# Stick-breaking attention: sums of softplus by matmul replaced by scans of sigmoids along rows, with the weights turned by TensorE

## What is computed

```
z = einsum('bhqd,bhsd->bhqs', q_blk, k) * HEAD_DIM ** -0.5
visible = arange(T)[None, :] < q_pos[:, None]
neg_log_1m_beta = where(visible, softplus(z), 0.0)
between = cumsum(neg_log_1m_beta, axis=3, reverse=True) - neg_log_1m_beta
weights = where(visible, exp(log_sigmoid(z) - between), 0.0)
out = einsum('bhqs,bhsd->bhqd', weights, v)
...
merged = sigmoid(gate_sb) * (o_sb @ w_branch_sb) + sigmoid(gate_rw) * (o_rw @ w_branch_rw)
h = h + rms_norm(merged @ w_out)
f = rms_norm(h); h = h + rms_norm((silu(f @ w_ffn_gate) * (f @ w_ffn_up)) @ w_ffn_down)
```

## Time and profile before

| | us |
|---|---|
| median of 3 runs | 879.5 (879.44 to 879.79) |
| the profiled execution | 879.9, its span 878.0 |
| PE busy | 862.6 (98%) |
| DVE busy | 487.1 (55%) |
| ACT busy | 411.1 (47%) |
| POOL busy | 94.1 (11%) |
| mixing stage on PE, from its first step to `u0.U` | 183.2 to 376.7 |

### The profile page before, as it was taken

How to read it: one execution, slowest core, us unless ns; L and a number is a source line. 1 busy time by engine, 2 the same in 40 slices (tenths; PEclk the granted TensorE clock), 3 DMA queues, 4 the chain that set the end, 5 groups by cost and what they waited for, 6 DMA issues and landing times.

```text
span 878.0 us, 18916 instructions
## 1 busy us (share of the span) xinstructions
PE 862.6 (98%) x8165; PEld 717.7 (82%) x8165; DVE 487.1 (55%) x642; ACT 411.1 (47%) x572; POOL 94.1 (11%) x92
## 2 busy tenths in 40 slices
PE   6999999999999999999999999999999999999997
PEld 5999999877777777767888898888888888888886
DVE  6459997346766666529675754444444444322333
ACT  6445565369777777555343643333333333211331
POOL 2015544111011101043100000000000000000000
PEclk9999999999999999999999999999999999999999
DMA  9332223321210011222367323333333333323311
GB/s 281 102 97 73 77 68 97 121 62 56 73 47 17 26 40 39 75 96 73 96 216 270 89 69 100 96 96 96 96 96 97 96 98 100 99 91 105 100 77 72
DMA packets 109584, 82.82 MB, mean 94 GB/s; under 512 B 3471, under 2 KB 100025, under 8 KB 109258
## 3 DMA queue, kind: packets, MB, share of 16 engines
q1 hardware_dynamic: 109514, 81.77, 30.4%
HBM read 75.99 MB, written 5.77 MB: 93 GB/s over the span
## 4 chain that ended last, share of the span: by engine, by line
PE 93%; DVE 4%; issue 1%; ACT 1%; DMA 0%; DVEq 0%; SPq 0%
PE psum L592 47%; PE psum L1899 19%; PE psum L1622 8%; PE psum L1678 7%; PE psum L1824 2%; PE psum L1942 2%; PE psum L1513 1%; PE psum L1834 1%; PE psum L1805 1%; DVE w_lo L582 1%; PE psum L1853 1%; DVE shift_diff L1184 1%; PE psum L1504 1%; DVE k_mod L1225 1%; DVE v_t L1189 1%
## 5 line engine op out<-in xcount | busy, mean ns | idle before, releaser
L582 DVE TENSOR_TENSOR w_lo<-w_raw,w_hi 128x1024 fp32r<-128x1024 f32 x69 | 88.9, 1289 | 120.7 <-ACT w_hi L577 116.3
L592 PE MATMUL psum<-f_hi,w_hi 128*128 128x512 f32 x336 | 130.8, 389 | 0.0
L592 PE MATMUL psum<-f_lo,w_hi 128*128 128x512 f32 x336 | 130.7, 389 | 0.0
L592 PE MATMUL psum<-f_hi,w_lo 128*128 128x512 f32 x336 | 130.7, 389 | 0.0
L1096 ACT ACTIVATE w_hi<-w_raw 128x1024 fp32r<-128x1024 f32 x44 | 46.7, 1061 | 166.7 <-PE psum L592 159.4
L1459 DVE TENSOR_TENSOR w_lo<-w_raw,w_hi 128x1024 fp32r<-128x1024 f32 x44 | 53.9, 1226 | 125.6 <-ACT w_hi L1096 121.4
L577 ACT ACTIVATE w_hi<-w_raw 128x1024 fp32r<-128x1024 f32 x70 | 73.7, 1054 | 74.7 <-PE psum L1899 56.1
L592 PE MATMUL psum<-h_hi,w_hi 128*128 128x264 f32 (+2 forms) x400 | 98.2, 310 | 0.8 <-DVE w_lo L582 0.8
L592 PE MATMUL psum<-h_lo,w_hi 128*128 128x264 f32 (+2 forms) x400 | 96.5, 306 | 0.0
L592 PE MATMUL psum<-h_hi,w_lo 128*128 128x264 f32 (+2 forms) x400 | 96.5, 306 | 0.0
L592 PEld LDWEIGHTS psum<-f_hi,w_hi 128*128 128x128 f32 x336 | 63.1, 188 | 13.2
(11 more groups left out here) (314 smaller groups left out, 1655.8 us busy)
## 6 DMA issues: line engine op xcount, KB each, us to landing
w_raw<-in_w_in SPq DMA_DIRECT2D x30, 512.0 KB, 3.7
w_raw<-in_w_g SPq DMA_DIRECT2D x22, 512.0 KB, 3.7
w_raw<-in_w_u SPq DMA_DIRECT2D x22, 512.0 KB, 3.8
w_raw<-in_w_d SPq DMA_DIRECT2D x22, 512.0 KB, 3.5
w_raw<-in_w_in SPq DMA_DIRECT2D x48, 128.0 KB, 2.2
w_raw<-in_w_out SPq DMA_DIRECT2D x8, 512.0 KB, 5.0
kept_gates<-gate_raw SPq DMA_DIRECT2D x10, 256.0 KB, 2.1
sig_t<-kept_gates SPq DMA_DIRECT2D x10, 256.0 KB, 2.8
```

The source lines that it names most:

```text
L582: nc.vector.tensor_sub(lo[:], raw[u % RAW][:], hi[:].bitcast(F32)).then_inc(w_split, 1)
L592: mm = nc.tensor.matmul(o, w[:, (w0 + i) * P:(w0 + i + 1) * P], xs[:, k, c0:c1], start=(n == 0), stop=(n == total - 1))
```

## The change

The scores are made with the queries on the partitions: `Q` takes `qT` as the stationary and `kT` as the moving operand, row i (128 queries) over its 16+128(i+1) keys. `kT` and the values are stored in reverse order of time. ACT writes sigmoid(z) into `stick` (`z`) and sigmoid(-z) into `rest` (`m`). POOL fills the invisible part with 0 in `stick` (`b`) and 1 in `rest` (`c`). DVE multiplies `rest` up along the row in place (`S`, one instruction for each row block and head), and multiplies with `stick` (`w`, and `t` for the meta keys into `smeta`). PE turns the weights block by block (`X0` to `X6`, in banks 4, 5 and 6), ACT copies them back into `rest` (`x0` to `x6`), and `O` follows as before. The triangles, softplus and its splits, and the steps `h` and `m0`, `m1` are gone. PIECES is 4 in place of 2. The four orders are written anew. Two set-up steps on POOL and one on DVE (`tri_r`) go, and `smeta` is zeroed on POOL.

```diff
-PIECES = 2
+PIECES = 4
...
+KEYS = [META + P * (i + 1) for i in range(QB)]
+ROW = {3: 0, 0: KEYS[3], 1: KEYS[3] + KEYS[0], 2: KEYS[3] + KEYS[0] + KEYS[1]}
+Q_COLS = ((0, SEQ), (ROW[2], ROW[2] + KEYS[2]), (SEQ, ROW[2]))
+TURNS = ((0, (0,)), (1, (0,)), (0, (1,)), (1, (1,)), (0, (2, 3)), (1, (2, 3)), None)
+T_BANKS = (4, 5, 6, 4, 5, 6, 5)
+O_BANK = 4
...
 ORDER_PE = order("""
-m0.Q i0.A i0.L s0.F a0.Q2 g0.G0 s0.T1 i0.W1 i0.R0 s0.T0 s0.T2 a0.Q1 g0.G1 i0.Y1 a0.Q0 i0.W2 i0.R1 s0.Z m1.Q
+a0.Q0 i0.A i0.L g0.G0 a0.Q1 i0.W1 s0.F i0.R0 a0.Q2 i0.Y1 g0.G1 i0.W2 i0.R1 g0.G2 s0.T0 i0.Y2 g0.G3 i0.W3 s0.T2
...
-s8.RB i4.Y4 h7.C4 a2.O s8.T2 i4.W5 i4.R4 s8.Z1 s8.Z i4.Y5 a3.O s8.SA u0.U s8.OUT1 s8.OUT
+i4.R3 g9.G1 s8.F i4.Y4 s8.RB a3.X6 a3.X5 i4.W5 a3.X3 i4.R4 s8.T2 g9.G2 s8.Z1 i4.Y5 s8.Z g9.G3 s8.SA a3.O s8.OUT1
+s8.OUT u0.U
...
 # POOL
+                    i = int(s[1])
+                    tile, src, fill = (stick, "z", 0.0) if s[0] == "b" else (rest[n % 2], "m", 1.0)
+                    d = tile[:, :, ROW[i]:ROW[i] + P]
+                    g.affine_select(out=d, in_=d, compare_op=ALU.is_gt, fill=fill, base=1 - P,
+                                    pattern=[[0, 2], [1, P]], channel_multiplier=1).then_inc(mix_pool, 1)
...
 # ACT
+                        c0, c1 = Q_COLS[j]
+                        tile, sign = (stick, 1.0) if s[0] == "z" else (rest[n % 2], -1.0)
+                        s_.activation(tile[:, :, c0:c1], psum[:, QBANKS[0]:QBANKS[0] + 2, 0:c1 - c0], ACT.Sigmoid,
+                                      scale=sign).then_inc(mix_act, 1)
+                    if s[0] == "x":
+                            s_.activation(rest[n % 2][:, hr, c0:c1], bank(T_BANKS[j], c1 - c0), ACT.Copy).then_inc(mix_act, 1)
...
 # DVE
+                    if s[0] == "S":
+                        row = rest[n % 2][:, int(s[2]), c0:c1]
+                        v_.tensor_tensor_scan(row, row, row, 1.0, ALU.mult, ALU.min).then_inc(mix_dve, 1)
+                        if s[0] == "w":
+                            w = stick[:, :, c0 + 1:c1 - META]
+                            v_.tensor_mul(w, w, rest[n % 2][:, :, c0:c1 - META - 1]).then_inc(mix_dve, 1)
...
 # PE
+                    if j:
+                        pe.wait_ge(mix_act, last_of(MIX_ACT, "att", n, (f"z{j - 1}", f"m{j - 1}")))
+                    elif n:
+                        pe.wait_ge(mix_act, last_of(MIX_ACT, "att", n - 1, [f"x{k}" for k in range(7) if T_BANKS[k] in QBANKS]))
+                    else:
+                        pe.wait_ge(in_out, N_IN)
...
+                    pe.wait_ge(mix_dve, last_of(MIX_DVE, "att", n, [f"{w}{i}" for w in "wt" for i in range(QB)]))
+                        for j in tiles:
+                            for i in range(j, QB):
+                                mm = t_.transpose(psum[:, T_BANKS[k], c0:c0 + P], stick[:, hr, r0:r0 + P], ident)
```

More of the change, by code:

```diff
@@ L188 @@
[L188 to L192, removed]
@@ L202 @@
[L202 to L206, removed]
@@ L234 @@
+s7.bh a3.b0
 """)
@@ L741, in _ @@
             g.memset(s_st[:], 0.0).then_inc(mix_zero, 1)
[L742 to L747 removed]
+            g.memset(smeta[:], 0.0).then_inc(mix_zero, 1)
             pool.wait_ge(mix_zero, N_ZERO)
@@ L865, in _ @@
                 elif kind == "sk":
-                    s_.activation(halves(kT[:, p, :]), ps, ACT.Copy).then_inc(in_out, 1)
+                    s_.activation(halves(kT[:, p, ::-1]), ps, ACT.Copy).then_inc(in_out, 1)
                 elif kind == "sv":
@@ L869, in _ @@
                         act.wait_ge(v_tp, p - 1)
-                    s_.activation(halves(vst[p % 2][:]), ps, ACT.Copy).then_inc(in_out, 1)
+                    s_.activation(halves(vst[p % 2][:, ::-1]), ps, ACT.Copy).then_inc(in_out, 1)
                 else:
@@ L1783, in _ @@
                     mm.then_inc(mix_pe, 1)
-                if kind == "meta":
-                    if n:
-                        pe.wait_ge(mix_act, upto(MIX_ACT, "att", 0, "z0"))
-                        pe.wait_ge(in_out, N_IN)
-                    for q in range(2):
-                        mm = t_.matmul(psum[64 * q:64 * q + 64, QBANKS[0], :], km[:, 2 * n + q, :], qT[:, 2 * n + q, :],
-                                       start=True, stop=True)
-                    mm.then_inc(mix_pe, 1)
@@ L1804, in _ @@
+                    spans = (((3, 0, SEQ),), ((2, 0, KEYS[2]),), ((3, SEQ, KEYS[3]), (0, 0, KEYS[0]), (1, 0, KEYS[1])))[j]
+                    for i, r0, r1 in spans:
+                        k0, c0 = T - KEYS[i], ROW[i] + r0 - Q_COLS[j][0]
                         for hr in range(2):
-                            mm = t_.matmul(psum[:, QBANKS[hr], c0:c0 + WIDTH[t]], kT[head(hr), n, k0:k0 + P],
-                                           qT[head(hr), n, SEQ - WIDTH[t]:SEQ], start=(t == j), stop=True,
+                            mm = t_.matmul(psum[:, QBANKS[hr], c0:c0 + r1 - r0], qT[head(hr), n, P * i:P * i + P],
+                                           kT[head(hr), n, k0 + r0:k0 + r1], start=(i == spans[0][0]), stop=True,
@@ new lines, in _ @@
+                if kind == "att" and s[0] == "X":
+                    k = int(s[1])
+                    pe.wait_ge(mix_dve, last_of(MIX_DVE, "att", n, [f"{w}{i}" for w in "wt" for i in range(QB)]))
+                    before = [q for q in range(k) if T_BANKS[q] == T_BANKS[k]]
+                    if before:
+                        pe.wait_ge(mix_act, upto(MIX_ACT, "att", n, f"x{before[-1]}"))
+                    elif T_BANKS[k] == O_BANK and n:
+                        pe.wait_ge(mix_act, upto(MIX_ACT, "att", n - 1, "o"))
+                    if TURNS[k]:
+                        hr, tiles = TURNS[k]
+                        for j in tiles:
+                            for i in range(j, QB):
+                                r0, c0 = ROW[i] + P * (i - j), OFF[j] - OFF[tiles[0]] + P * (i - j)
+                                mm = t_.transpose(psum[:, T_BANKS[k], c0:c0 + P], stick[:, hr, r0:r0 + P], ident)
+                    else:
+                        for i in range(QB):
+                            mm = t_.transpose(psum[0:64, T_BANKS[k], P * i:P * i + P],
+                                              smeta[:, i].rearrange("p h k -> p (h k)"), ident)
@@ L1837, in _ @@
                     mm.then_inc(mix_pe, 1)
                 if kind == "att" and s == "O":
[L1839 to L1845 removed]
+                    pe.wait_ge(mix_act, last_of(MIX_ACT, "att", n, [f"x{k}" for k in range(7)]))
@@ L1852, in _ @@
                             v0 = (2 * n + hr) * HD
-                            mm = t_.matmul(psum[head(hr), QBANKS[1], SEQ - WIDTH[j]:SEQ], vtok[:, j, v0:v0 + HD],
-                                           zs[n % 2][:, hr, OFF[j]:OFF[j] + WIDTH[j]], start=False, stop=(j == QB - 1))
+                            mm = t_.matmul(psum[head(hr), O_BANK, SEQ - WIDTH[j]:SEQ], vtok[:, j, v0:v0 + HD],
+                                           rest[n % 2][:, hr, OFF[j]:OFF[j] + WIDTH[j]], start=False, stop=(j == QB - 1))
                     mm.then_inc(mix_pe, 1)
```

293 lines of the change are left out of this document (80 added, 213 removed).

## The result

The changed kernel takes 864.97 us, the median of 4 runs (863.89 to 865.3), against 879.64 (879.44 to 880.62) of the kernel before on the same chip: ratio 0.9829, interval 0.9812 to 0.9846, about 15 us less. The profiled execution took 863.89 us, its span is 861.9 against 878.0.

The account below looks back on a forecast made before the run. PE's own work was taken to set the mixing stage's length; removed and added PE terms summed to -10.65 us, from 879.5 to 868.9, stated as 868.5 us for unpriced small borders, with a range of 862 to 875.

Parts of the forecast that it names:

- Removed: PE, mixing stage: the triangle sum steps (29.3 us) and meta score steps (2.0) go, -31.3 us; -0.9 more for borders.
- Transposes: PE, `X` groups: turned blocks overlap, 3.3 us a pair, +13.2 us; rival without overlap 26.1 us, chance 0.05.
- Scores: PE, `Q` steps: 3.15 us a pair in place of 2.76, in all +1.6 us, between +0.4 and +2.5.
- Gate borders: PE, gates in four pieces: 55 more borders between fp32r and fp32 at 0.105 us each, +5.8 us.
- Start: PE, stage's start: a0.Q0 must wait for ACT's copy of the last projection, +0.85 us.
- Waits of the new orders: PE, all chains of the new lists: +0.6 us in all, 0.4 of it at a0.Q2, the first `X` tightest.
- ACT without table loads in the stage: Sign to look for in the changed profile: ACT makes no function table loads in the mixing stage.
- End: PE, stage's end: u0.U is last and hides ACT's last copy and osb_hi, -0.5 us.
- Inverses: PE, inverse steps: distances between chained steps mostly as long as before; no separate gain in the sum.
- The other engines cost nothing: ACT, DVE, POOL: edits covered by PE's gates and RWKV steps; all under two thirds of a 182 us stage.
- DVE at twice the price: Rival: PE waits for attention's DVE chain, first `X` 5.5 us late; +5.5 to +9 us, 874 to 877.5, chance 0.12.
- 2.38 ns an element: DVE scans: 1258 ns for 528 elements, so eight heads of 1344 elements take 25.6 us.

Follow-up runs that it names:

- turn_twice: The changed kernel with every transpose of the weights issued twice into the same place, 96 more: 875.3 us, ratio 0.9942 to the kernel before.
- gates_in_two: The changed kernel with each gate unit's second piece right behind the first and the fourth behind the third: 876.32 us, ratio 0.9949 to the kernel before.
- start: The changed kernel with i0.A and i0.L ahead of a0.Q0 on PE and an early one-column sigmoid on ACT: 862.07 us, ratio 0.9785 to the kernel before.
- openings_close: The changed kernel with 14 openings (Z1, OUT1) set back directly ahead of their full steps: 869.52 us, ratio 0.9867 to the kernel before.
- scan_twice: The changed kernel with each DVE scan made a second time into a spare row: 879.25 us, ratio 0.9976 to the kernel before.
- one_table: The kernel before with Sigmoid in place of Exp and Ln in attention, so one function table on ACT: ratio 0.9998 to the kernel before.
- end_early: The kernel of `start` with s8.OUT1 ahead of a3.O instead of behind it in PE's list: 865.55 us, ratio 0.9822 to the kernel before.
- openings_apart: The kernel before with the step ahead of each of 12 close opening pairs exchanged with the opening: 884.17 us, ratio 1.0036 to the kernel before.

## Why the prediction was right, step by step

The mechanism and the sign were right, and 864.97 us lies within the range and the forecast's own 864 to 873. It is 3.5 us below the 868.5: a gain of 11.0 us was forecast, 14.7 was measured, and 16.0 between the profiled executions. The terms, as predicted and as measured:

- *Removed*, -31.3 and -0.9 (borders), together -32.2: measured -30.1 - 2.3 = -32.4.
- *Transposes*, +13.2: measured +12.1, and 0.109 us each in turn_twice. The price of a group's start, some 0.12 us by the earlier trace rows, was too high: 12.1 / 96 is 0.126 each, and 12.1 - 96 x 0.109 leaves 0.06 for each of the 28 groups.
- *Scores*, +1.6: measured +1.2. A pair takes 1.06 + 0.87 + 1.13 us, the last step 0.09 less than the 1.22 priced, in which 0.3 stood for the 16 columns without a row; they took 0.2.
- *Gate borders*, 55 x 0.105 = +5.8: measured +4.7, 0.085 each, and 0.092 in gates_in_two. The number of borders was right; the price came from two pieces of the earlier trace rows alone.
- *Start*, +0.85: measured about +0.9. `start` shows that it could be had back.
- *Waits of the new orders*, +0.6: measured 1.4, both at the first scores. The step that failed is "ACT without table loads in the stage", which the text on the change also says: one is left, ahead of the first sigmoid, and with its 1.28 us it is longer than the wait of 0.97 us behind it. The first `X`, which I held for the tightest place, has no wait.
- *End*, -0.5, and nothing for the scan's other steps: measured -3.1 for the scan. This is the largest error. Of 12 openings directly ahead of their full step two are left, 0.2 us each, and I had not looked at the waits of the weight loads, where the row stood. openings_close gives 2.9 us back for 14 pairs. Of the other 1.0 us, 0.7 fits the wait of 0.48 at the end, which went, with its drain; that part was not tested alone.
- *Inverses*, nothing: measured -0.9, some 0.6 of it the place in `i3.Y2` where PE stood still before. It is a third row of waits before, 0.4 us, beside the two that I read. Not tested.
- *The other engines cost nothing*: right for this kernel, since PE's whole wait for them is 2.1 us. But "all stay under two thirds of the stage" is no reason for it. In scan_twice DVE stays under two thirds and the stage is 15.4 us longer, more than my rival gave for DVE at twice the price (+5.5 to +9), and the waits are not at the first `X`, where I had put them, but at the inverse and the scan.
- *The 2.38 ns an element* of the scan held for 528 elements (1266 ns), not for 144 (512 ns, 3.6 each); the eight heads took 28.0 us in place of 25.6, without effect.
- *`u0.U` near 367 us*: it started at 362.88, earlier because the sum was too small. The places differ too: before, it ran ahead of `OUT1` and `OUT`, and after behind them.

The Trainium skill ("TensorE: Matmul & The Clock Gate", Part 4: PE-mode transpose) gives about 275 ns for a transpose; the trace agrees with that as the duration of one (273 ns), and differs as to the price, 0.109 us by turn_twice. With 96 of them between the other steps the clock stayed at 1.00.

The sum was -10.65 us and the stage shows -16.2. The missing 5.5 us are errors of nearly one sign (scan 2.6, transposes 1.1, gate borders 1.1, inverses 0.9, scores 0.4, removed steps 0.2, against 0.8 of waits the other way). So the time did not come right by errors that cancel: it is within the range because that reached 6.5 us below the forecast. With the terms of the table in their place the sum is -16 us.

## What to carry to other kernels

Where one engine is busy for 98% of a stage, price what a change takes from and adds to that engine from start to start in its timeline; relief of ACT was worth nothing here (one_table), but work added to another engine costs nothing only so long as no step of another chain stands behind it in its queue (scan_twice). Cutting filler work into more pieces costs borders and can be worth several times that, if they are what stands between a producer and its consumer. Before moving a step in such an order, list every producer it needs, on all engines, and read the waits of the weight loads too.

## What was not expected of the hardware

- *A short wait costs more than itself.* Behind waits of 1.09 us (end_early) and 1.85 us (openings_apart) a window of 5 us shows a granted clock of 0.66 and 0.67, the lower level for the greater part of it, and 1.09 us became 2.7. Yet the waits of 0.3 to 1.2 us in gates_in_two left the stage's clock at 1.00, and so did 0.97 us at the start of the changed kernel. The length of the wait alone does not decide it: in scan_twice waits of 2.07 and 2.79 us were followed by the lower clock, and this one of 2.21 us was not:

```profile
252.42 0.45 PE L1589 MATMUL psum<-x_inv,aab 32*32 32x32 f32 x32 [2.21 <-DVE x_inv L1227]
```

```profile
240.00:270.00 30.00, 27.53 (x807) 21.02 (x796) 21.91 (x37) 10.80 (x22) 8.72 (x10) 1.00 0.13 38
```

What tells these cases apart was not tested.
- *A step that must wait for PE's own step right ahead of it waits 0.2 us* (12 and 16 times, above). The wait is written in the kernel; one step in between hides it.
- *A border between fp32r and fp32 costs 0.085 to 0.092 us* at the gate's side, by 55 and by 40 of them.
- *Scans in place*: 2.4 ns an element at 528, 3.6 at 144.
- *PE stands still inside a step* for 0.4 to 1.2 us once in the stage of several traces, without a named releaser.
